# The second tile's instruction order, the place of its output product, and separate buffers for even experts' down weights

## The chip, the cores and the metric

The kernel runs on one core of a Trainium2 chip. The metric is the device time of one execution in microseconds (us), the median of several executions. The engines of the core are TensorE (PE in the rows, PEld for its weight loads), VectorE (DVE), ScalarE (ACT), GpSimd (POOL) and SyncE (SP), which here only issues DMA.

## The reference

One residual stream of 256 tokens with 1024 channels goes through two blocks. The first block ends in a product-key retrieval (128 picked rows per token). The second block is a hybrid layer:

```
def hybrid_layer(x, c, ...):
    mods = jax.nn.silu(c) @ w_ada + b_ada
    h = rms_norm(x, norm1_g) * (1.0 + scale1) + shift1
    proj = h @ w_in                                   # 1824 + 1536 columns
    y_rwkv = rwkv7_time_mix(proj[..., :RWKV_PROJ], ...)  # 8 heads of 64, a scan over tokens
    y_moba = moba_attention(proj[..., RWKV_PROJ:], ...)  # 8 heads of 64, causal softmax
    x = x + gate1 * (jnp.concatenate([y_rwkv, y_moba], axis=-1) @ w_out)
    h = rms_norm(x, norm2_g) * (1.0 + scale2) + shift2
    y = moe_ffn(h, ...)     # 32 experts, top 4 of them per token, each 1024 -> 2048 -> 1024
    return x + gate2 * y
```

Everything is float32. All 32 experts' weights are read once: 8 MB of gate and up weights and 4 MB of down weights for each.

## The kernel before

The 256 tokens are two tiles of 128 rows. Weights stream from HBM in chunks of 1 MB through a ring of 12 slots (`ring`); SP issues every chunk in the order in which TensorE uses it, and waits with each for the chunk that had the slot before (`chunk_done`, counted by TensorE).

The first tile's second block runs between the picks of the second tile's retrieval. When the last pick is done, the second tile's block runs alone: this is the stretch from 912 us to 1104 us, called the bare stretch below. Its work is three programs per engine, written as Python generators that yield the name of their next step: `attention` (steps mb, msum, mscore, mturn, att: the projections for attention, the sums for the norm of q and k, scores, turning of the probabilities, product with v), `mixer` (steps rw, lora, ksum, bonus, gup: its projections and small products; tok, gram, nt: products inside chunks of 32 tokens; pow and inv: powers of a matrix and its inverse; z1, wu, q2, yp, fg, gam: what the scan over chunks needs; st: the scan; ys, ln: output and norm; or: its half of the output product; turn4, route: the router) and `output` (om: the half of the output product that reads attention's result). `to_end` (L205) always takes the program whose next step stands first in the list `ORDER` (L190). So `ORDER` alone sets the order of an engine's instructions in the bare stretch, and since each engine works in order, an instruction that waits holds up all behind it.

In the bare stretch of the kernel before, the rw projections come first, the mb projections stand among the mixer's powers and inverses, the softmax stands beside the scan, and om stands among ln.

After the bare stretch comes the loop over 32 experts (`expert` on TensorE, L2215): 8 gate-up chunks (L2235), gathering the next expert's tokens (L2195), bias rows (L2206), 4 down chunks (L2265), and scattering (L2277). TensorE's first expert waits also for a transfer of bias rows (`loaded_b`, awaited after L2186, issued by ACT at L982 behind its last step of the second tile). SP loads: gate-up of expert 0 into the ring, its four down chunks into `first_dn`, four free pieces of the work buffer `arena`; the down chunks of expert 1 into the ring; then the gate-up of 1, the gate-up and down of 2, of 3, and so on, each chunk into the ring slot that the same chunk of the expert before had.

Of the kernel before, what the change touches and what calls it, by code (L numbers as in the profile page):

```python
# [58 lines left out]


# [24 lines left out]
def stream_order():  # L85
# [103 lines left out]
ORDER = """sum norm gain norm1 xn turn xres rw0.0 rw0.1 rw1.0 rw1.1 mixl rw2.0 rw2.1 loin rw3.0 lora rw3.1 sigw mixk scan rw4.0 rw4.1 ksum kn  # L189
rw5.0 rw5.1 exps mixr kmod rw6.0 rw6.1 rkk rw7.0 bonus rw7.1 mixv gup kk mb0.0 tilde mb0.1 bon mb1.0 mb1.1 tok gram0 gram1  # L190
gram2 gram3 nt mb2.0 pow1 mb2.1 inv1 pow2 mb3.0 inv2 mb3.1 pow3 mb4.0 inv3 mb4.1 pow4 mb5.0 mb5.1 inv4 msq z1 msum wu rms qk
q2 mscore0 yp mscore1 fg0 fg1 fg2 fg3 gam0 gam1 gam2 gam3 soft exp st0 prob st1 mturn0 st2 mturn1 st3 att ys om0 ln1 om1 ln2
om2 ln3 om3 or0 or1 or2 or3 norm2 turn4 route""".split()
# [60 lines left out]
def build(nc, xd, stream, colsd, matsd, rowsd, badad, expert_uv, w_gate_up, w_down, bias_moe, out):  # L254
    with ExitStack() as ctx:
# [149 lines left out]
        first_dn = [area(at, CHUNK) for at in (2048, 4096, 16384, 18432)]  # L405
# [1957 lines left out]
```

## Time and profile before

| | |
|---|---|
| median of 3 executions | 2050.06 us (2047.68 to 2053.04) |
| the profiled execution | 2048.01 us, span 2046.2 us |
| TensorE, VectorE, ScalarE busy | 1767.4, 961.6, 485.8 us |
| HBM read | 770.53 MB, 377 GB/s over the span |
| bare stretch | 912 to 1104 us |
| expert loop | 1104 us to the end |

The span is what the profiler saw of the program; the execution's own time has 1.8 us more around it. The busy shares are means over stages with different limits. In the page's slices the transfers run at 400 to 422 GB/s in most of the program, fall to 42 GB/s in the slices of the bare stretch, and run at 422 GB/s from 1150 us to the end.

### The profile page before, as it was taken

To read this page: it belongs to the slowest core of one execution; us is meant where nothing else is said; L and a number is where in the kernel's file an instruction comes from. 1 tells how busy PE (TensorE), PEld (TensorE's weight loads), DVE (VectorE), ACT (ScalarE), POOL (GpSimd) and SP (SyncE) were. 2 spreads that over 40 slices of the span, in tenths; PEclk is the share of its full clock that TensorE was granted. 3 is DMA by queue.
4 is the path that set the end of the run, shared out by engine and by line. 5 is a ranking of instruction groups with operands and counts; after the bars stand their busy time and mean duration, and the time that the engine had idled before them with its cause. 6 is when DMAs were issued, how large, how long until landed. Compare 5 with 4: busy or idle time off the path is not lost.

```text
span 2046.2 us, 27368 instructions
## 1 busy us (share of the span) xinstructions
PE 1767.4 (86%) x10376; PEld 841.8 (41%) x10376; DVE 961.6 (47%) x2029; ACT 485.8 (24%) x1183; POOL 288.9 (14%) x286
## 2 busy tenths in 40 slices
PE   7999988566688888769967999999999999999997
PEld 6888544111145454318854333333333233333322
DVE  4755877788556776554452223222232232223223
ACT  1111443334345543433221011110111011111101
POOL 1000433334442444320000000000000000000000
PEclk9999998766699998869978999999999999999999
DMA  9982999999999999998217899999999999999997
GB/s 387 388 349 110 387 421 420 421 421 419 420 400 420 413 421 396 367 365 352 91 42 281 347 422 422 422 422 422 422 422 422 422 422 422 422 422 422 422 422 319
DMA packets 107047, 772.69 MB, mean 378 GB/s; under 512 B 12148, under 2 KB 12404, under 8 KB 13272
## 3 DMA queue, kind: packets, MB, share of 16 engines
q1 hardware_dynamic: 69408, 500.51, 59.3%
q0 software_dynamic: 36864, 268.45, 32.0%
q10 hardware_dynamic: 696, 2.66, 0.3%
q8 instruction: 51, 0.84, 0.2%
q14 instruction: 28, 0.23, 0.0%
HBM read 770.53 MB, written 1.05 MB: 377 GB/s over the span
## 4 chain that ended last, share of the span: by engine, by line
PE 50%; DMA 30%; DVE 9%; ACT 4%; SPq 3%; issue 3%; POOL 1%; DVEq 0%; POOLq 0%; ACTq 0%
DMA ring<-in_expert_uv,arena 15%; DMA ring<-in_w_gate_up 14%; PE psum L2235 14%; PE psum L2265 7%; PE psum L1854 6%; PE psum L1706 4%; SPq L605 3%; DVE ring L1275 2%; PE psum L2277 2%; PE psum L1811 2%; PE psum L1956 2%; PE psum L1789 1%; PE psum L1895 1%; PE psum L1774 1%; PE psum L2140 1%
## 5 line engine op out<-in xcount | busy, mean ns | idle before, releaser
L2235 PE MATMUL psum<-ring,arena 128*64 128x512 f32 x2048 | 458.8, 597 | 24.1 <-DMA ring<-in_w_gate_up 22.6
L1854 PE MATMUL psum<-ring,arena 64*64 64x512 f32 x2048 | 348.9, 767 | 145.2 <-ACT arena L837 143.9
L1275 DVE CUSTOM_DVE_ANT_0 ring<-ring,arena 128x1024 f32<-128x1024 f32 x256 | 312.0, 1225 | 164.6 <-DMA ring<-in_expert_uv,arena 162.0
L704 POOL DMA_INDIRECT ring<-in_expert_uv,arena x256 | 278.3, 1087 | 605.5 <-PE psum L1854 399.9
L2235 PEld LDWEIGHTS psum<-ring,arena 128*64 128x64 f32 x2048 | 138.7, 137 | 339.8 <-issue 256.2
L2265 PE MATMUL psum<-ring,arena 128*64 128x512 f32 x992 | 219.7, 595 | 0.6
L1651 DVE TENSOR_SCALAR arena<-psum 128x512 f32<-128x512 f32 x32 | 22.1, 692 | 401.2 <-PE psum L2235 401.2
L1854 PEld LDWEIGHTS psum<-ring,arena 64*64 64x64 f32 x2048 | 64.7, 155 | 349.7 <-ACT arena L837 327.8
L997 ACT ACTIVATE arena<-arena 128x512 f32<-128x512 f32 x32 | 20.2, 630 | 760.2 <-DVE arena L1651 760.2
L828 ACT ACTIVATE arena<-arena 128x1 f32<-128x1 f32 x256 | 51.7, 202 | 328.5 <-DVE arena L1275 328.2
L2265 PEld LDWEIGHTS psum<-ring,arena 128*64 128x64 f32 x992 | 68.5, 137 | 131.9 <-issue 123.9
L1706 PE MATMUL psum<-arena,ring 128*128 128x256 f32 x512 | 111.6, 379 | 0.0
L1660 DVE TENSOR_TENSOR arena<-psum,gates 128x512 f32<-128x512 f32 x32 | 22.1, 691 | 189.4 <-PE psum L2265 189.4
L1706 PEld LDWEIGHTS psum<-arena,ring 128*128 128x128 f32 x512 | 97.0, 190 | 13.2 <-issue 0.4
L1663 DVE TENSOR_TENSOR xres<-xres,psum 128x1024 f32<-128x1024 f32 x64 | 75.3, 1218 | 40.8 <-PE psum L2277 40.8
L837 ACT ACTIVATE arena<-arena 128x64 f32<-128x64 f32 x256 | 89.0, 348 | 8.3
L2277 PE MATMUL psum<-arena 64*128 64x512 f32 x256 | 63.6, 612 | 26.9 <-issue 26.9
L832 ACT ACTIVATE arena<-arena,peer_g 128x1 f32<-128x1 f32 x256 | 75.4, 294 | 8.8
L1811 PEld LDWEIGHTS psum<-arena,ring 128*128 128x128 f32 x512 | 61.2, 197 | 25.3 <-issue 25.3
L1811 PE MATMUL psum<-arena,ring 128*128 128x128 f32 x512 | 66.8, 286 | 0.9 <-ACT arena L737 0.9
L2195 PE MATMUL psum<-arena 128*64 128x512 f32 x264 | 63.8, 605 | 3.3 <-DMA arena<-in_bias_moe 3.3
L1956 PEld LDWEIGHTS psum<-arena,ring 128*128 128x128 f32 x448 | 53.8, 199 | 13.0 <-issue 10.2
(360 smaller groups left out, 1716.7 us busy)
## 6 DMA issues: line engine op xcount, KB each, us to landing
ring<-in_w_gate_up SPq DMA_DIRECT2D x256, 1024.0 KB, 24.8
ring<-in_w_down SPq DMA_DIRECT2D x124, 1024.0 KB, 23.9
ring<-in_stream SPq DMA_DIRECT2D x91, 1024.0 KB, 10.9
ring<-in_expert_uv,arena POOLq DMA_INDIRECT x256, 13.0
arena<-in_w_down SPq DMA_DIRECT2D x4, 1024.0 KB, 6.3
mats<-in_mats ACTq DMA_DIRECT2D x1, 1152.0 KB
xres<-in_x SPq DMA_DIRECT2D x2, 512.0 KB, 4.1
arena<-in_rows ACTq DMA_DIRECT2D x2, 512.0 KB, 7.7
```

What stands on the lines that cost most here:

```text
L704: pool.indirect_dma_start(ring[:, G_SLOTS[b], :], None, expert_uv, bass.IndirectOffsetOnAxis(peer_i[:, tt, k:k + 1], 0)).then_inc(row_in[b ...
L832: act.activation(peer_w[:, 0, c % 4:c % 4 + 1], one, ACT.Copy, scale=peer_g[:, tt, k:k + 1]).then_inc(weight_step, 1)
L837: act.activation(diag[:, c % 4, :], ident2, ACT.Copy, scale=peer_w[:, 0, c % 4:c % 4 + 1]).then_inc(diag_ready, 1)
L1275: dve.tensor_tensor_reduce(u, u, h2[tt], 1.0, 0.0, ALU.mult, ALU.add, peer_h[:, tt, k:k + 1]).then_inc(dot_done, 1)
L1663: dve.tensor_tensor(xres[:, tt, :], xres[:, tt, :], psum[:, (6, 3)[tt]:(8, 5)[tt], :].rearrange("p a c -> p (a c)"), ALU.add).then_inc(acc ...
L1706: last = pe.matmul(psum[:, bank, c * T:(c + 1) * T], wide(n)[:, k, c * P:(c + 1) * P], acts[:, k, :], start=(k == 0), stop=(k == KD - 1))
L1811: last = pe.matmul(psum[:, bank, o:o + P], wide(n)[:, k, cs], h2T[:, k, ts], start=(k == 0), stop=(k == KD - 1), skip_group_check=True)
L1854: last = pe.matmul(psum[o:o + 64, 6 * tt + h, :], diag[rows, c % 4, :], rows_of[b][rows, 1, h * 512:(h + 1) * 512], start=(k == 0), stop=( ...
L1956: last = pe.matmul(half[:, c * P:(c + 1) * P], wide(n)[:, k, c * P:(c + 1) * P], hT3[tt][:, k, :], start=(k == 0), stop=(k == KD - 1), ski ...
L2235: last = pe.matmul(psum[CAP * h:CAP * h + CAP, gu, :], x, w[:, at:at + 512], start=False, stop=(kt == GU_CHUNKS - 1), skip_group_check=True)
L2265: last = pe.matmul(psum[CAP * h:CAP * h + CAP, 5, :], a_in, w[:, i * D + h * 512:i * D + h * 512 + 512], start=False, stop=(kt == KD - 1), ...
L2277: last = pe.matmul(psum[:, (6, 3)[tt] + h, :], sct[rows, tt, :], ye[rows, :], start=True, stop=True)
```

## The change

1. For the second tile the mb projections stream and run before the rw projections, and attention's remaining steps stand between the rw projections.
2. The second tile's om steps stand between the powers and the inverses. Its output product uses PSUM banks 6 and 7 (`OUT_BANK`) where it had 4 and 5, and its wait for `fg_out` goes. Several buffers of the second tile lie elsewhere in `arena` or `mats`.
3. Down chunks of every even expert go to four fixed buffers `more` (the pieces that `first_dn` had), those of odd experts to ring slots. SP issues the chunks in this order: gu0, dn0, dn1, then gu1, dn2, gu2, dn3, gu3, and so on, where gu and dn are the gate-up and the down chunks. TensorE's loop body has two experts.
4. The bias rows' transfer is issued by ACT inside the mixer's step ln2 of the second tile.

```diff
-        seq += rw + mb if tt else mb + rw
-        seq += [("o2", i, tt) for i in range(N_O2)]
+        seq += mb + rw + [("o2", i, tt) for i in range(N_O2)]
...
-ORDER = """sum norm gain norm1 xn turn xres rw0.0 rw0.1 rw1.0 rw1.1 mixl rw2.0 ...
+ORDER = """sum norm gain norm1 xn turn xres mb0.0 mb0.1 mb1.0 mb1.1 mb2.0 ...
...
-            expert(0, 0, range(GU_CHUNKS))
+            gates_ups(0, 0)
             sp.wait_ge(pv_mm, TT)
-            sp.wait_ge(yp_mm, TT)
-            sp.wait_ge(fg_mm, 4 * TT)
             for q in range(DN_CHUNKS):
                 if q == 2:
-                    sp.wait_ge(chunk_done, AT["o2", 0, TT - 1] + 1)
-                down(0, q, first_dn[q]).then_inc(landed_first, 16)
-            expert(1, 0, range(GU_CHUNKS, E_CHUNKS))
-            expert(1, E_CHUNKS, range(GU_CHUNKS))
-            with sp.Fori(2, NE) as e:
-                expert(e, e * E_CHUNKS, range(E_CHUNKS))
+                    sp.wait_ge(fg_mm, 4 * TT)
+                down(0, q, more[q]).then_inc(landed_more[q], 16)
+            for q in range(DN_CHUNKS):
+                n = C_MOE + GU_CHUNKS + q
+                sp.wait_ge(chunk_done, n - SLOTS + 1)
+                down(1, q, slot(n)).then_inc(landed[slot_of(n)], 16)
+            with sp.Fori(0, NE // 2 - 2) as i:
+                for odd in (1, 0):
+                    e = 2 * i + (2 - odd)
+                    gates_ups(e, e)
+                    downs(e + 1, e + 1, 1 - odd)
+            gates_ups(NE - 3, NE - 3)
+            downs(NE - 2, NE - 2, 0)
+            gates_ups(NE - 2, NE - 2)
+            gates_ups(NE - 1, NE - 1)
+            downs(NE - 1, NE - 1, 1)
...
                 yield "ln2"
                 act.wait_ge(ln_mm, 2 * tt + 2)
+                if tt:
+                    act.dma_start(bmoe[0:3 * NE], bias_moe).then_inc(loaded_b, 16)
...
             to_end([started(attention(1)), started(mixer(1))])
-            act.dma_start(bmoe[0:3 * NE], bias_moe).then_inc(loaded_b, 16)
...
                         pe.wait_ge(ym_ready, tt + 1)
-                        pe.wait_ge(fg_out, 4 * (tt + 1))
+                        if tt == 0:
+                            pe.wait_ge(fg_out, 4)
...
-                if isinstance(p, int):
-                    expert(0, 0)
-                with pe.Fori(1 if isinstance(p, int) else 0, NE) as e:
-                    expert(p * NE + e, p * (NE + 1) + e)
+                with pe.Fori(0, NE // 2) as i:
+                    for odd in range(2):
+                        expert(p * (NE // 2) + i, p * (NE + 1) + (2 * i + odd), odd)
```

The line numbers of the changed kernel are up to 22 higher than before for the same code. In TensorE's order of the kernel before, the bare stretch begins with the rw projections (L1956, L1961), with lora (L1969), ksum (L1977) and bonus (L1982) between them:

```order
L1956 MATMUL psum<-arena,ring 128x128 x16
L1961 MATMUL psum<-arena,ring 32x128 x8
L1956 MATMUL psum<-arena,ring 128x128 x32
L1969 MATMUL psum<-arena,mats 128x128 x8
L1956 MATMUL psum<-arena,ring 128x128 x32
L1977 MATMUL psum<-arena,headblk 128x512
L1956 MATMUL psum<-arena,ring 128x128 x32
L1982 MATMUL psum<-arena,headblk 128x512
```

In the changed kernel the mb projections come first (16 and 64 matmuls, not shown), then the same place of TensorE reads as follows; L1977 and L1982 are now rw, L1923 msum, L1935 mscore, L1990 lora, L1946 mturn, L1998 ksum:

```order
L1977 MATMUL psum<-arena,ring 128x128 x16
L1923 MATMUL psum<-arena,headblk 128x512 x2
L1982 MATMUL psum<-arena,ring 32x128 x8
L1935 MATMUL psum<-arena 128x256 x4
L1977 MATMUL psum<-arena,ring 128x128 x8
L1935 MATMUL psum<-arena 128x256 x4
L1977 MATMUL psum<-arena,ring 128x128 x24
L1990 MATMUL psum<-arena,mats 128x128 x8
L1977 MATMUL psum<-arena,ring 128x128 x16
L1946 MATMUL psum<-ident,arena 128x128 x8
L1977 MATMUL psum<-arena,ring 128x128 x8
L1946 MATMUL psum<-ident,arena 128x128 x8
```

The scores and the turning of the probabilities have moved from beside the scan to between the rw projections. TensorE's powers and inverses before, with half mb chunks (L1895) between pow (L2036, L2041) and inv (L2050):

```order
L1895 MATMUL psum<-arena,ring 128x128 x8
L2036 MATMUL psum<-arena 128x128 x4
L2041 MATMUL psum<-arena 128x128 x4
L2036 MATMUL psum<-arena 128x128 x4
L2041 MATMUL psum<-arena 128x128 x4
L1895 MATMUL psum<-arena,ring 128x128 x8
L2050 MATMUL psum<-arena 128x128 x8
```

The same place in the changed kernel, where L2189 is om, L2057 and L2062 pow, L2071 inv:

```order
L2041 MATMUL psum<-arena 128x128 x8
L2057 MATMUL psum<-arena 128x128 x4
L2062 MATMUL psum<-arena 128x128 x4
L2057 MATMUL psum<-arena 128x128 x4
L2062 MATMUL psum<-arena 128x128 x4
L2189 MATMUL psum<-ring,arena 128x256 x4
L2071 MATMUL psum<-arena 128x128 x8
```

One om step now stands between each power and its inverse. On ScalarE, the softmax exponential (L856) before stands directly behind the copy of yp (L939):

```order
L851 ACTIVATE arena<-psum,stat 128x1024
L853 ACT_TABLE_LOAD
L853 ACTIVATE arena<-arena 128x1024
L939 COPY arena<-psum 128x512
L856 ACTIVATE arena<-arena 128x2048
L862 COPY arena<-psum 128x1024 x2
```

In the changed kernel it is L876, and stands behind the copy of an rw chunk pair (L908) and the eight sigmoids of sigw (L926), which read lora's result:

```order
L919 ACTIVATE arena<-arena 32x128
L908 COPY arena<-psum 128x4x128
L926 ACTIVATE arena<-psum,cols 128x128 x8
L876 ACT_TABLE_LOAD
L876 ACTIVATE arena<-arena 128x2048
L882 COPY arena<-psum 128x1024 x2
```

A load of the activation table now stands between the sigmoids and the exponential.

## Rows read from the trace of the kernel before

**Rows 1.** Windows: microseconds, then busy time (instructions) by engine, clock, DMA share, GB/s.
```profile
1025.00:1050.00 25.00, 10.54 (x246) 9.19 (x242) 17.62 (x27) 2.50 (x2) 0.00 (x0) 0.64 0.01 1
...
1500.00:2000.00 500.00, 464.46 (x2250) 154.24 (x2252) 136.43 (x237) 57.76 (x85) 0.00 (x0) 1.00 1.01 422
```

**Rows 2.** Chain of waits, expert loop: start, duration, what.
```profile
1103.82 13.98 PE psum L2235 x64
...
1122.04 7.09 PE psum L2265 x32
...
1131.96 13.91 PE psum L2235 x64
```

**Rows 3.** Windows around the first expert.
```profile
1125.00:1130.00 5.00, 4.16 (x22) 1.21 (x18) 0.69 (x1) 0.00 (x0) 0.00 (x0) 1.00 0.46 192
1130.00:1135.00 5.00, 5.00 (x24) 1.83 (x26) 3.35 (x7) 0.00 (x0) 0.00 (x0) 1.00 0.00 0
1135.00:1140.00 5.00, 5.00 (x26) 1.67 (x24) 0.00 (x0) 0.00 (x0) 0.00 (x0) 1.00 0.89 310
```

**Rows 4.** Timeline, TensorE: start, duration, line, shapes, records; in brackets idle before and releaser.
```profile
926.56 5.25 PE L1956 MATMUL psum<-arena,ring 128*128 128x128 f32 x32 [2.20 <-ACT arena L880]
...
942.03 7.41 PE L1956 MATMUL psum<-arena,ring 128*128 128x128 f32 x64
...
961.51 7.17 PE L1891 MATMUL psum<-ring,arena 128*128 128x256 f32 x32
968.52 1.91 PE L1999 MATMUL psum<-ident,arena 128*128 128x128 f32 x16
...
979.30 1.16 PE L2036 MATMUL psum<-arena 128*128 128x128 f32 x8 [0.97 <-DVE arena L1476]
...
1013.71 1.99 PE L1902 MATMUL psum<-arena,headblk 128*128 128x512 f32 x4 [0.25 <-DVE arena L1288]
...
1023.59 1.14 PE L1914 MATMUL psum<-arena 64*128 64x256 f32 x8 [2.50 <-DVE arena L1293]
...
1038.80 1.94 PE L2113 MATMUL psum<-mats,arena 128*128 128x64 f32 x8 [5.69 <-issue]
...
1056.60 3.24 PE L1934 MATMUL psum<-arena 128*64 128x128 f32 x32 [1.10 <-ACT arena L862]
1059.77 0.42 PE L2124 MATMUL psum<-arena,mats 64*64 64x32 f32 x8
...
1061.75 2.00 PE L2167 MATMUL psum<-ring,arena 128*128 128x256 f32 x8
...
1073.36 8.61 PE L2140 MATMUL psum<-ring,arena 128*128 128x256 f32 x32 [2.60 <-DVE arena L1551]
...
1097.23 3.39 PE L2195 MATMUL psum<-arena 128*64 128x512 f32 x8 [3.33 <-DMA arena<-in_bias_moe]
```

**Rows 5.** Timeline, ScalarE.
```profile
942.13 2.17 ACT L906 ACTIVATE arena<-psum,cols 128x128 f32<-128x128 f32 x8 [0.50 <-PE psum L1969]
...
1016.86 1.28 ACT L853 ACT_TABLE_LOAD   x1
1018.16 1.06 ACT L853 ACTIVATE arena<-arena 128x1024 f32<-128x1024 f32 x1
...
1043.38 1.91 ACT L856 ACTIVATE arena<-arena 128x2048 f32<-128x2048 f32 x1 [14.81 <-DVE arena L1310]
```

**Rows 6.** Timeline, VectorE.
```profile
1045.32 2.29 DVE L1314 TENSOR_REDUCE gsm<-arena 128x8 f32<-128x2048 f32 x1 [1.19 <-ACT arena L856]
...
1053.83 0.42 DVE L1527 TENSOR_TENSOR arena<-psum,arena 128x256 f32<-128x256 f32 x1 [2.87 <-PE psum L2113]
...
1094.53 0.42 DVE L1612 TENSOR_SCALAR arena<-iota_slot,arena 128x64 f32<-128x64 f32 x2
```

**Rows 7.** Windows of 5 us: the clock where TensorE resumes.
```profile
1025.00:1030.00 5.00, 5.00 (x110) 4.23 (x107) 1.83 (x6) 0.58 (x1) 0.00 (x0) 0.66 0.00 0
...
1050.00:1055.00 5.00, 4.78 (x23) 4.78 (x24) 1.78 (x5) 1.01 (x1) 0.00 (x0) 0.50 0.00 0
```

More of the change, by code:

```diff
@@ L58 @@
 FG_BANK = (4, 5, 1, 2)
+OUT_BANK = (4, 6)
 N_Z = D_IN // CW
@@ L186 @@
 assert max(SLOT.values()) < PICKS
[L189 to L193, printed above, removed]
+ORDER = """sum norm gain norm1 xn turn xres mb0.0 mb0.1 mb1.0 mb1.1 mb2.0 mb2.1 mb3.0 mb3.1 mb4.0 mb4.1 mb5.0 mb5.1 msq
+rw0.0 rw0.1 msum rms rw1.0 qk rw1.1 mixl mscore0 rw2.0 loin mscore1 rw2.1 lora sigw soft rw3.0 rw3.1 exp mixk rw4.0 prob rw4.1
+scan ksum kn mturn0 rw5.0 mturn1 rw5.1 exps mixr kmod att rw6.0 rw6.1 rkk rw7.0 bonus rw7.1 kk tilde mixv gup bon tok gram0
+gram1 gram2 gram3 nt pow1 om0 inv1 pow2 om1 inv2 pow3 om2 inv3 pow4 om3 inv4 z1 wu q2 yp fg0 fg1 fg2 fg3 gam0 gam1 gam2 gam3
+st0 st1 st2 st3 ys ln1 ln2 ln3 or0 or1 or2 or3 norm2 turn4 route""".split()
 RANK = {s: i for i, s in enumerate(ORDER)}
@@ L403, in build @@
         gmoe = gates[:, 1, 0:512]
-        first_dn = [area(at, CHUNK) for at in (2048, 4096, 16384, 18432)]
+        more = [area(at, CHUNK) for at in (16384, 18432, 2048, 4096)]
         xs = area(6144, W2)
@@ L608, in down, with gates_ups @@
                 return sp.dma_start(dst, w_down[e, q * 2 * P:(q + 1) * 2 * P, :].rearrange("(p k) c -> p (k c)", k=2))
-            def expert(e, before_it, js):
-                for j in js:
+            def gates_ups(it, e):
+                for j in range(GU_CHUNKS):
                     n = C_MOE + j
-                    sp.wait_ge(chunk_done, before_it + (n - SLOTS + 1))
-                    if j < GU_CHUNKS:
-                        ins = gate_up(e, j, slot(n))
-                    else:
-                        ins = down(e, j - GU_CHUNKS, slot(n))
-                    ins.then_inc(landed[slot_of(n)], 16)
@@ L623, in _, with downs @@
-            expert(0, 0, range(GU_CHUNKS))
+                    sp.wait_ge(chunk_done, it * E_CHUNKS + (n - SLOTS + 1))
+                    gate_up(e, j, slot(n)).then_inc(landed[slot_of(n)], 16)
+            def downs(it, e, odd):
+                for q in range(DN_CHUNKS):
+                    n = C_MOE + GU_CHUNKS + q
+                    sp.wait_ge(chunk_done, it * E_CHUNKS + (n - 2 * E_CHUNKS + 1))
+                    if odd:
+                        down(e, q, slot(n)).then_inc(landed[slot_of(n)], 16)
+                    else:
+                        down(e, q, more[q]).then_inc(landed_more[q], 16)
@@ new lines, in _ @@
+            for q in range(DN_CHUNKS):
+                n = C_MOE + GU_CHUNKS + q
+                sp.wait_ge(chunk_done, n - SLOTS + 1)
[8 more added lines that the diff above has]
+            gates_ups(NE - 2, NE - 2)
@@ L636, in experts @@
+            gates_ups(NE - 1, NE - 1)
+            downs(NE - 1, NE - 1, 1)
             def experts(p):
-                with sp.Fori(0, NE) as e:
-                    expert(e, e * E_CHUNKS + p * (NE * E_CHUNKS), range(E_CHUNKS))
+                with sp.Fori(0, NE // 2) as i:
+                    for odd in range(2):
+                        gates_ups(p * NE + (2 * i + odd), 2 * i + odd)
+                        downs(p * NE + (2 * i + odd), 2 * i + odd, odd)
             further_passes(sp, experts)
@@ L2139, in mixer @@
                     for k in range(4):
-                        last = pe.matmul(psum[:, 4 + n // 2, (n % 2) * CW:(n % 2 + 1) * CW], yT[tt][:, k, :],
+                        last = pe.matmul(psum[:, OUT_BANK[tt] + n // 2, (n % 2) * CW:(n % 2 + 1) * CW], yT[tt][:, k, :],
                                          wide(AT["o2", n, tt])[:, k, :], start=False, stop=(k == 3), skip_group_check=True)
```

33 lines of the change are left out of this document (17 added, 16 removed).

## The prediction

> **What bounds the kernel now.** I read the windows first. In the expert loop the transfers run at 422 GB/s without a hole [rows 1], so from there on HBM sets the pace. A 1 MB chunk then takes 1.0486 MB / 422 GB/s = 2.485 us, an expert's twelve 29.8 us. The chain of waits shows TensorE's own pace, which is faster: first gate-up matmul of expert 0 at 1103.82, of expert 1 at 1131.96, so 28.14 us each [rows 2]. In the bare stretch the transfers nearly stop (0.01 of the engines' time between 1025 and 1050 [rows 1]): the buffers for weights are full and free up only when TensorE reaches expert 0. So the end is the moment T0 of expert 0's first matmul (1103.8 before), plus the holes in the transfers after T0, plus a fixed number of chunks, plus a tail (last down chunk, scatter, store) that the change leaves as it is. Everything before 923 us is also left as it is. Two questions remain: what happens to T0, and to the holes.
>
> **The hole behind T0.** Before T0, 16 chunks are loaded (gu0, dn0, dn1) in both kernels. From T0 on gu1 follows as gu0 is consumed. Before, gu2 stood next, and had to wait for gu1's slots, thus until T0 + 28.1 + 1.75: the windows show the transfers ending near 1127.3 (0.46 of 1125 to 1130), none from 1130 to 1135, and a start near 1135.55 (0.89 of the next) [rows 3]. The hole is 8.25 us. In the changed kernel dn2 stands behind gu1 and goes where dn0 was, which TensorE consumes from 1122.04, that is T0 + 18.2 [rows 2]: its first chunk is free at T0 + 20, before gu1 is in at T0 + 23.5. Its four chunks take 9.9 us, until T0 + 33.4, and by T0 + 29.9 gu2 may start. The hole closes: -8.25 us. After that TensorE's slack only grows (1.7 us per expert), so the 16 buffers bring nothing more. The loop body of two experts costs or saves nothing while HBM sets the pace.
>
> **T0: the bare stretch, leg by leg.** TensorE is the engine to follow; the section on the change has its order. Times are on the clock of the trace before; both kernels start at 926.56.
>
> Leg 1, to tok. Before, tok starts at 968.52 [rows 4]. Now:
> - mb: two chunks of v 7.1 (their row), plus 1.6 which the first 32 records lost at the low clock (5.25 where 3.65 is normal); four of k and q at 3.65, less overlap 14.3; rw0 3.7: 953.3 [rows 4].
> - msum to mscore. Before, msum started at 1013.71 and mscore at 1023.59, but VectorE was held there by other work. Without that: Ln ready 2.0 + 1.1, table load and Exp 2.4, VectorE 1.5: 7.05 [rows 4, 5]. So mscore0 starts at 960.35; only 1.9 us of rw1 lie in it, TensorE idles 3.4.
> - mscore0, rw2.0, a wait of 0.7 for VectorE's reading of the scores, mscore1: 965.0. rw2.1 to rw3.1 5.4, lora 1.1, rw4 3.6: 975.1.
> - mturn0 needs the probabilities. The scores are reduced and ready for the exponential at 971.2, but on ScalarE it stands behind sigw: lora starts at 970.4, its first result allows sigw at 971.6, sigw takes 2.2, the table load 1.3, Exp 1.9: 977.0 [rows 5]. VectorE's reduce, reciprocal, multiply: 4.9 (from 1045.32 to TensorE's next at 1050.2) [rows 6]. So mturn0 starts at 982.0, and behind it all of TensorE's queue (rw5 to gup) has waited 6.9 us.
> - mturn, rw5, ksum, att 3.2 (L1934), rw6, rw7, bonus, gup: 22.7. After such an idle stretch the granted clock was 0.50 to 0.66 of full speed for the next 5 us or more [rows 7], and full again before 10 us of work; I take 2.5 us for it (bounds 0 and 4.4). ScalarE's copy of gup's result 0.7: tok at 1007.9. That is +39.4.
>
> Leg 2, tok to the first scan step. Before 968.52 to 1038.80, 70.3 us [rows 4]. Now tok to pow1 10.8 as before (968.52 to 979.30, VectorE's masks set it). A level of powers is 3.6 of pow and 1.8 of inv, and om's 1.75 stands between them. I looked for slack there and found none: pow's copies are ready when inv wants them, so om's four steps cost their full 7 us, where before, between ln steps (1061.75 on), they lay in waits and cost about 0.3. Three levels of 7.2 and one of 5.4: 27.0. z1 and its copy 2.7, wu 4.5, q2 1.0, yp 3.2, fg 4.1, gam 5.5. From z1 on these are the distances in TensorE's timeline before, without mscore's share. Sum 58.8: the scan starts at 1066.7. That om no longer waits for `fg_out` and has banks of its own is what lets it stand here, and is worth nothing by itself.
>
> Leg 3, the scan to ys (L2124). Before 1038.80 to 1059.77, 21.0 us, because softmax, turning and att stood in it. Now three steps of 1.85 + 0.87 + 0.1 (1051.98 to the next VectorE row at 1053.83, and its two operations) [rows 6]: 8.5. ys at 1075.2.
>
> Leg 4, ys to or. Before 1059.77 to 1073.36, 13.6 us [rows 4]. TensorE now comes to it from 15 us of little work, without om between, and so at the low clock: ys, two sums for the norm and the first of or lengthen. 13.6 - 0.3 + 2.5 = 15.8 (bounds 13.3 and 17): or at 1091.0.
>
> Leg 5, or to T0. Before 30.5 us. The bias rows landed at 1097.23, while the one-hot rows that L2195 also needs were written by 1094.95 [rows 4, 6]: moving the transfer up is worth 2.3 us and no more; its issue (0.1 to 0.3) now stands ahead of ln2's Ln. The low clock adds 0.8 to or. 29.2: T0 at 1120.2, so +16.4.
>
> In short, and roughly: stalls removed beside the scan and softmax are worth 12.5 in leg 3, and are paid for by attention's 6.8 us of products moved ahead, om's 7, two new stalls of 3.4 and 6.9, 1.8 of filler gone from gram, and clock. The bounds on T0 are +10.5 (no clock cost at all: 2.5, 2.5 and 0.8 less) and +20 (both clock terms at their upper ends).
>
> **The sum.** 2048.0 (the profiled execution) + 16.4 - 8.25 = 2056.2. The median of the runs shown is 2.0 above that execution: 2058. Transfers do not spoil it: the second tile's output chunks are in by 970, long before om, and dn1 is in 12 us after or starts, with 29 us until T0.
>
> At the table load the trace shows the next activation 0.02 us behind the load's 1.28 [rows 5], and I used that. The Trainium skill (ScalarE: Activation LUTs, What ACT_TABLE_LOAD costs) adds a drain of about 1.38 us to each switch. By that rule the load that now stands before the softmax exponential, on the path, would cost 1.4 us more, an estimate of 2059.6; the trace disagrees with it here.
>
> **Rivals.**
> - No measurable change. The clock does not matter: the windows mix idle time and low clock, and the small products of leg 4 may be bound by their fixed cost. Then T0 is +10 to +12, the sum 2050 + 2 to +4: 2053. For it: the products of leg 4 are few and stand between VectorE's steps. Against: 0.50 in every row where TensorE resumed late [rows 7]. Chance 0.27.
> - Faster. What is bought: TensorE's waits of 5.69 before the scan, 2.50 and others beside softmax (about 21 us between 1013 and 1062) go, and the new ones do not appear: if probabilities are ready before rw4 ends, 10.3 of stalls and 2.5 of clock go from my sum, and if om finds 7 us of slack in the powers, that too. T0 is -3, and with the hole 2058 - 20 = 2038. It decides at mturn0: the exponential would have to end by 970. Against: ScalarE's order puts sigw first, and no duration in the chain is uncertain by more than tenths. Chance 0.09.
> - Much slower. TensorE's clock stays low through rw5 to gup and from the scan until T0: another 5 to 10 us, 2066. Chance 0.05.
>
> **How the numbers follow.** My case 0.59, at 2058, its own range 2054 to 2062. Range 2049 to 2064. About 0.3% (6 us) can be told from no change: slower means above 2056.2. Of my case 0.57 lies above it and 0.02 below; with the last rival slower is 0.62. Same is 0.27 + 0.02 = 0.29, faster 0.09.
>
> **What the changed profile would show.** TensorE: a wait of about 7 us before the first mturn (L1946), one of 3.4 before the first mscore (L1935); no idle time around om (L2189) among the powers, and pow1 to z1 27 us; the scan's three steps in 8.5 us; expert 0's first matmul near 1120, 16 later. Transfers: no window without traffic between T0 + 5 and T0 + 40. No wait for the bias rows. I am wrong in the mechanism if the exponential starts before lora's sigmoids or T0 is earlier than 1112; wrong in the loop if a hole remains, or if the end does not follow T0.

## The result: slower by 1.3%, outside the range

| | before | after |
|---|---|---|
| median | 2048.87 us (4 executions, 2047.01 to 2053.04) | 2074.94 us (4 executions, 2073.31 to 2078.73) |
| the profiled execution | 2048.01 | 2078.73 |
| bare stretch, first projection to T0 | 926.56 to 1103.82 = 177.3 | 927.87 to 1132.67 = 204.8 |
| T0 to TensorE's last group (scatter of expert 31) | 933.2 | 933.4 |
| T0 to the end of the span | 942.4 | 944.2 |
| mean clock in the bare stretch | 0.87 | 0.78 |

The ratio is 1.0127 (95% interval 1.0105 to 1.0149). The forecast was 2058 with a range up to 2064. The profiled execution is the slowest of its four, 3.8 us above their median, so sizes read from it are a little large.

The profile has two places to read. The first is the bare stretch: TensorE's timeline after, with start, duration, line, shapes and records, and in brackets the idle time before and its releaser. These rows answer to [rows 4].

```profile
927.87 9.42 PE L1912 MATMUL psum<-ring,arena 128*128 128x256 f32 x32 [2.20 <-ACT arena L900]
...
961.89 1.14 PE L1935 MATMUL psum<-arena 64*128 64x256 f32 x8 [3.16 <-DVE arena L1314]
...
984.67 1.97 PE L1946 MATMUL psum<-ident,arena 128*128 128x128 f32 x8 [6.60 <-DVE arena L1337]
...
1010.58 3.68 PE L2020 MATMUL psum<-ident,arena 128*128 128x128 f32 x16 [3.36 <-DVE arena L1471]
...
1023.20 1.16 PE L2057 MATMUL psum<-arena 128*128 128x128 f32 x8 [2.95 <-DVE arena L1497]
...
1042.67 1.89 PE L2189 MATMUL psum<-ring,arena 128*128 128x256 f32 x8
1044.40 1.95 PE L2071 MATMUL psum<-arena 128*128 128x128 f32 x16
...
1055.44 0.64 PE L2088 MATMUL psum<-arena 128*128 128x64 f32 x2
...
1073.95 1.94 PE L2134 MATMUL psum<-mats,arena 128*128 128x64 f32 x8 [5.64 <-issue]
...
1083.09 3.62 PE L2145 MATMUL psum<-arena,mats 64*64 64x32 f32 x64 [1.07 <-DVE mats L1550]
...
1091.90 2.07 PE L2155 MATMUL psum<-arena,headblk 128*128 128x512 f32 x2 [1.59 <-DVE arena L1562]
1101.69 9.54 PE L2161 MATMUL psum<-ring,arena 128*128 128x256 f32 x32 [7.72 <-DVE arena L1572]
...
1124.79 3.68 PE L2217 MATMUL psum<-arena 128*64 128x512 f32 x8 [1.19 <-DVE arena L1633]
1128.40 2.00 PE L2228 MATMUL psum<-arena 32*64 32x512 f32 x12
...
1132.67 3.65 PE L2257 MATMUL psum<-ring,arena 128*64 128x512 f32 x16 [1.67 <-DVE arena L1650]
```

The two stalls that the prediction named are there, before mscore (L1935, 3.16) and before mturn (L1946, 6.60). So is om (L2189) among the powers with no wait beside it. Nobody waits for the bias rows: L2217 waits 1.19 for VectorE. New are the 3.36 before tok (L2020), and the length of everything at the end: TensorE waits 7.72 before or (L2161) where it waited 2.60, or took 9.54 where it took 8.61, L2217 3.68 for 3.39 and L2228 2.00 for 1.10.

The windows after (microseconds, busy time by engine, clock, DMA share, GB/s) show the clock that goes with it; compare the clock of [rows 7].

```profile
1050.00:1055.00 5.00, 4.12 (x38) 4.02 (x37) 2.07 (x3) 0.00 (x0) 0.00 (x0) 1.00 0.00 0
1055.00:1060.00 5.00, 5.00 (x27) 5.00 (x26) 0.69 (x1) 0.00 (x0) 0.00 (x0) 0.53 0.02 3
...
1095.00:1100.00 5.00, 0.00 (x0) 0.00 (x0) 1.62 (x5) 4.55 (x5) 0.00 (x0) 0.50 0.27 78
1100.00:1105.00 5.00, 3.31 (x8) 2.68 (x9) 1.57 (x3) 0.00 (x0) 0.00 (x0) 0.50 0.00 0
...
1125.00:1130.00 5.00, 5.00 (x20) 0.93 (x18) 1.06 (x6) 1.73 (x3) 0.00 (x0) 0.50 0.00 0
...
1155.00:1160.00 5.00, 4.16 (x22) 1.50 (x20) 0.69 (x1) 0.00 (x0) 0.00 (x0) 1.00 1.00 415
1160.00:1165.00 5.00, 5.00 (x26) 1.62 (x24) 3.35 (x7) 0.00 (x0) 0.00 (x0) 1.00 1.01 421
```

The granted clock is at its lower level (0.50, which is 1.2 of 2.4 GHz) in most windows from 1055 to 1130. The last two rows are the place that answers to [rows 3], 22 to 32 us behind T0: the transfers run at 415 and 421 GB/s there. The hole of 8.25 us is gone. Yet from T0 on nothing was gained: the end is 1.8 us later. For that, the second place: TensorE at the loop's end, after.

```profile
2023.53 1.94 PE L2257 MATMUL psum<-ring,arena 128*64 128x512 f32 x8 [0.54 <-DMA ring<-in_w_gate_up]
...
2039.73 13.95 PE L2257 MATMUL psum<-ring,arena 128*64 128x512 f32 x64
...
2066.02 1.99 PE L2299 MATMUL psum<-arena 64*128 64x512 f32 x8 [0.84 <-issue]
```

And the same place before:

```profile
1993.03 1.94 PE L2235 MATMUL psum<-ring,arena 128*64 128x512 f32 x8 [0.54 <-DMA ring<-in_w_gate_up]
...
2009.15 10.69 PE L2235 MATMUL psum<-ring,arena 128*64 128x512 f32 x48
2020.38 1.94 PE L2235 MATMUL psum<-ring,arena 128*64 128x512 f32 x8 [0.54 <-DMA ring<-in_w_gate_up]
2022.86 1.94 PE L2235 MATMUL psum<-ring,arena 128*64 128x512 f32 x8 [0.55 <-DMA ring<-in_w_gate_up]
...
2037.06 1.99 PE L2277 MATMUL psum<-arena 64*128 64x512 f32 x8 [0.84 <-issue]
```

Before, TensorE waits for the last gate-up chunk of expert 31 (2022.86), 14.2 us ahead of its last group, the scatter. After, its last wait is for the last gate-up chunk of expert 30 (2023.53), and from there TensorE's own pace sets the 42.5 us to the scatter: expert 31's 64 matmuls run without a wait. Before, the same way took 44.0, so TensorE had 1.5 us of slack there. In the new order dn30 stands ahead of gu30, and every gate-up from expert 2 on is four chunks (9.9 us) later in the queue. Measured from T0, the last chunk of gu30 came at 1993.03 - 1103.82 = 889.2 before and at 2023.53 - 1132.67 = 890.9 after: -8.25 for the hole, +9.94 for the four chunks, +1.69 in all. The slack takes 1.5 of it, and the scatter starts 0.1 later, at T0 + 933.4 for 933.2.

The rest of the 1.8 is the store of the output, which SP issues in

```profile
2070.77 0.83 SPq L663 DMA_DIRECT2D out<-xres  x2
```

after, 6.1 us ahead of the span's end, and before in

```profile
2041.81 0.83 SPq L643 DMA_DIRECT2D out<-xres  x2
```

4.4 us ahead of it. From the scatter to the end of the span it is 9.1 to 10.5 us in the five kernels of this document with the old loads, and 9.9 to 11.1 in the eight with new ones. Whether the loads or chance make this difference is not settled.

### The profile page after: what moved, and what is told of

Its sections match the earlier page's. It is cut to its first block, busy times and chain, and to the rows that moved or that the text cites. A ratio compares the mean times of both kernels' runs of the same rounds, so it can differ in the third digit from the quotient of the medians.

```text
span 2076.9 us, 27251 instructions
## 1 busy us (share of the span) xinstructions
PE 1779.7 (86%) x10376; PEld 854.7 (41%) x10376; DVE 962.2 (46%) x2029; ACT 485.4 (23%) x1183; POOL 286.9 (14%) x286
## 4 chain that ended last, share of the span: by engine, by line
PE 51%; DMA 28%; DVE 9%; ACT 5%; issue 3%; SPq 3%; POOL 0%; ACTq 0%; DVEq 0%; POOLq 0%
DMA ring<-in_expert_uv,arena 15%; DMA ring<-in_w_gate_up 14%; PE psum L2257 14%; PE psum L2287 7%; PE psum L1727 5%; PE psum L1875 5%; SPq L609 3%; DVE ring L1296 2%; PE psum L2299 2%; PE psum L1832 2%; PE psum L1977 2%; PE psum L1810 1%; PE psum L1916 1%; PE psum L1795 1%; PE psum L2161 1%
## 5 line engine op out<-in xcount | busy, mean ns | idle before, releaser
L2257 PE MATMUL psum<-ring,arena 128*64 128x512 f32 x2048 | 457.1, 597 | 23.6 <-DMA ring<-in_w_gate_up 21.9
L2257 PEld LDWEIGHTS psum<-ring,arena 128*64 128x64 f32 x2048 | 138.9, 137 | 337.3 <-issue 263.6
L2287 PE MATMUL psum<-arena 128*64 128x512 f32 x512 | 113.4, 595 | 1.6
L2287 PE MATMUL psum<-ring,arena 128*64 128x512 f32 x512 | 113.4, 595 | 1.5
L1727 PEld LDWEIGHTS psum<-arena,ring 128*128 128x128 f32 x512 | 96.8, 190 | 13.3 <-issue 0.4
L1832 PEld LDWEIGHTS psum<-arena,ring 128*128 128x128 f32 x512 | 61.0, 196 | 24.8 <-issue 24.8
L2217 PE MATMUL psum<-arena 128*64 128x512 f32 x264 | 64.0, 607 | 1.2 <-DVE arena L1633 1.2
L2287 PEld LDWEIGHTS psum<-arena 128*64 128x64 f32 x512 | 36.5, 137 | 68.1 <-issue 68.1
## 6 DMA issues: line engine op xcount, KB each, us to landing
ring<-in_stream SPq DMA_DIRECT2D x91, 1024.0 KB, 10.5
```

The costliest lines, as they stand in the source:

```text
L1727: last = pe.matmul(psum[:, bank, c * T:(c + 1) * T], wide(n)[:, k, c * P:(c + 1) * P], acts[:, k, :], start=(k == 0), stop=(k == KD - 1))
L1832: last = pe.matmul(psum[:, bank, o:o + P], wide(n)[:, k, cs], h2T[:, k, ts], start=(k == 0), stop=(k == KD - 1), skip_group_check=True)
L2217: last = pe.matmul(psum[CAP * h:CAP * h + CAP, 2, :], oh[:, tt, :], xn4[:, tt, h * 512:(h + 1) * 512], start=(tt == 0), stop=(tt == TT - 1))
L2257: last = pe.matmul(psum[CAP * h:CAP * h + CAP, gu, :], x, w[:, at:at + 512], start=False, stop=(kt == GU_CHUNKS - 1), skip_group_check=True)
L2287: last = pe.matmul(psum[CAP * h:CAP * h + CAP, 5, :], a_in, w[:, i * D + h * 512:i * D + h * 512 + 512], start=False, stop=(kt == KD - 1), ...
```

## Experiments

Times are medians; ratios are to the kernel before in the same batch, with 95% intervals. 1 us is 0.0005. The changed kernel ran in the batch of the result alone, so differences to it compare medians across batches; the kernel before had 2048.87 there, 2049.01 with e1 to e4, 2048.73 with e5 to e9 and 2047.81 with e10 to e12. Stretch means first projection to T0 in the profiled execution, "to the end" T0 to the end of the span, "to the scatter" T0 to TensorE's last group.

**e1_loop_only and e2_loop_switch: does the loop's change lose its gain to the place of the down chunks?** e1 is the kernel before with part 3 of the change alone. e2 closes the hole in the same way, but SP goes back to gate-up first in the middle of the loop:

```
-            with sp.Fori(0, NE // 2 - 2) as i:      # e1, as in the change
+            with sp.Fori(0, 7) as i:                # e2
                 for odd in (1, 0):
                     e = 2 * i + (2 - odd)
                     gates_ups(e, e)
                     downs(e + 1, e + 1, 1 - odd)
...
+            gates_ups(15, 15)
+            with sp.Fori(8, NE // 2) as i:
+                for odd in range(2):
+                    gates_ups(2 * i + odd, 2 * i + odd)
+                    downs(2 * i + odd, 2 * i + odd, odd)
```

> The kernel before with part 3 of the change alone (down chunks of even experts in their own buffers, SP's new order, loop body of two experts). Both theories leave the bare stretch and the first expert's start as they are. Recorded theory (only the hole counts): the hole of 8.25 us behind the first expert closes and the rest is fixed, so 8 us faster, 2041. New theory (end of the loop): the hole closes, but every gate-up from expert 2 on now stands behind the four down chunks of its own expert, 4 x 2.49 = 10.0 us of transfer that was behind it before. From the arrival of expert 30's last gate-up chunk TensorE alone needs 53 us to the end, so the end moves by 10.0 - 8.25 = +1.7: 2050.6, from 0 to 3 us slower.

> As the kernel with part 3 alone, but SP returns at expert 16 to the order gate-up of an expert, then its down chunks (gate-up of 15, gate-up of 16, down of 16, gate-up of 17, down of 17, ...). New theory: the hole stays closed, and at the end a gate-up has no down chunk of its own ahead of it; the limit is again expert 31's last gate-up chunk, 23.3 us before the end: 7 to 8 us faster than the kernel before, 2041. Recorded theory: 2041 too, and the same as part 3 alone. A third possibility, that the closed hole is lost elsewhere (TensorE's loop, contention): the same as part 3 alone, at 2049 or later.

Measured: e1 2051.35, ratio 1.0015 [1.0001, 1.0029], 945.2 to the end, 934.9 to the scatter. e2 2043.01, ratio 0.9972 [0.9959, 0.9985], 936.2 to the end, 926.4 to the scatter. The recorded theory that the closed hole gives 8 us fell with e1; the new theory's times held for e1 and nearly for e2 (6 us gained, 7 to 8 expected). Its 53 us from gu30's last chunk to the end are TensorE's 42.5 and the way from the scatter to the end; it left out the 1.5 of slack. At the end of the loop of e2, the last gate-up chunk of expert 31 is again the last wait:

```profile
2018.54 1.94 PE L2254 MATMUL psum<-ring,arena 128*64 128x512 f32 x8 [0.57 <-DMA ring<-in_w_gate_up]
```

It is at T0 + 912.1, where before it was at 2022.86 - 1103.82 = 919.0: 6.9 earlier, not 8.25. In both profiled executions the granted clock was low in the first microseconds behind T0 (0.50 from 1107.5 to 1110 in e2), and expert 0's 64 gate-up matmuls took 15.65 us instead of 13.95; SP's first chunk behind T0 was issued at T0 + 3.4 in e2 and T0 + 3.3 in e1, where before it was T0 + 2.0. That accounts for the missing 1.4. The same delay is in e1's 934.9, where the changed kernel has 933.4. In e10 below, which has e2's loads and took 13.95 for these matmuls, the scatter is at T0 + 924.8, 8.5 earlier than before: the whole hole. So the early down chunks are worth 6 us by medians if the order goes back once the hole is behind, and nothing if it stays.

**e3_bias_only: part 4 alone.**

```
                 yield "ln2"
...
+                if tt:
+                    act.dma_start(bmoe[0:3 * NE], bias_moe).then_inc(loaded_b, 16)
...
-            act.dma_start(bmoe[0:3 * NE], bias_moe).then_inc(loaded_b, 16)
```

> The kernel before with part 4 alone (the bias rows' transfer issued inside ln2). Recorded theory: 2.3 us of waiting gone less 0.1 to 0.3 for the issue: 2 us faster, 2047. New theory: ScalarE's table load for Ln, which before was done while it waited for ln2's sum, now stands behind the issue of the transfer, on the path: 0.34 + 1.28 later there, so only 0.7 us faster, 2048, and a trace in which the load of L942's table starts after the transfer's issue. The hole in the transfers stays 8.25 us.

Measured: 2050.45, ratio 1.0010 [0.9997, 1.0022]. Stretch 179.7, which is 2.4 longer than before. ScalarE in e3:

```profile
1067.97 0.34 ACTq L943 DMA_DIRECT2D arena<-in_bias_moe  x1
1068.34 1.28 ACT L944 ACT_TABLE_LOAD   x1 [7.25 <-PE psum L2135]
1069.64 0.69 ACT L944 ACTIVATE arena<-psum,stat 128x512 f32<-128x512 f32 x1
```

and before, where the load of Ln's table is over before its data is there:

```profile
1060.49 1.28 ACT L942 ACT_TABLE_LOAD   x1
...
1067.35 0.69 ACT L942 ACTIVATE arena<-psum,stat 128x512 f32<-128x512 f32 x1 [5.58 <-PE psum L2134]
```

The issue stands behind the wait for the sum of the norm, and the table load behind the issue. Both are now on the path: or in e3 is

```profile
1075.64 9.75 PE L2141 MATMUL psum<-ring,arena 128*128 128x256 f32 x32 [4.26 <-DVE arena L1552]
```

It waits 4.26 for VectorE where it waited 2.60 [rows 4], 1.66 more, and then runs 9.75 long at the low clock where it ran 8.61. These two are 2.8 us. The gather behind then waits 1.19 for VectorE instead of 3.33 for the bias rows, 2.1 less, but it and the bias rows' products take 3.68 and 2.00 instead of 3.39 and 1.10, 1.2 more. So nothing is gained. Both expectations, 2 and 0.7 us faster, missed, the second narrowly: the interval reaches from 0.6 us faster to 4.5 slower. By the Trainium skill (ScalarE: Activation LUTs, What ACT_TABLE_LOAD costs) a drain of about 1.38 us would follow the load; here the activation starts 0.02 us behind it.

**e4_order_only: parts 1 and 2 alone.** The changed kernel's `ORDER`, stream order, banks and buffers, with the loads, the loop and the bias rows of before:

```
+OUT_BANK = (4, 6)
...
-        seq += rw + mb if tt else mb + rw
-        seq += [("o2", i, tt) for i in range(N_O2)]
+        seq += mb + rw + [("o2", i, tt) for i in range(N_O2)]
```

> The changed kernel with the loads and the loop of the kernel before (its experts' order, first_dn) and the bias rows issued where they were: parts 1 and 2 alone. Recorded theory: the bare stretch is 18.5 us longer (16.4 + 2.3 - 0.2), 2067. New theory from the trace of the changed kernel: the order costs all that was measured, +26 less what parts 3 and 4 do (+1.7 and -0.7), so +25: 2074. Both expect the loop behind the first expert as before.

Measured: 2068.58, ratio 1.0095 [1.0077, 1.0112], stretch 200.2, 943.2 to the end. The order costs 19.5 us (15.8 to 22.9). That is the recorded theory's 18.5; the new theory's 25 fell. In the profiled execution the stretch is 22.9 longer than before, but it began 3.5 earlier; its start lies anywhere from 921.7 (e1) to 928.5 (e11) in the profiled executions, which the medians carry too. With e1's 3 and e3's 2 the parts sum to about 25 of the 26 measured.

e4 also shows what part 4 does once the order has changed. Its bias rows are issued where they were before, behind or, and still nobody waits for them:

```profile
1094.00 8.60 PE L2141 MATMUL psum<-ring,arena 128*128 128x256 f32 x32 [6.05 <-DVE arena L1552]
...
1115.71 3.68 PE L2197 MATMUL psum<-arena 128*64 128x512 f32 x8 [1.19 <-DVE arena L1613]
```

Their transfer landed 4.4 us after its issue, against 9.6 in the kernel before. So the wait of 3.33 that part 4 was to remove was gone by the order alone. What was left of part 4 is its price: in the changed kernel TensorE waits 7.72 before or for 6.05 here, and or takes 9.54 for 8.60.

**e5_om_back: does om cost its full 7 us among the powers?** The changed kernel, om back at ys and ln:

```
- gram1 gram2 gram3 nt pow1 om0 inv1 pow2 om1 inv2 pow3 om2 inv3 pow4 om3 inv4 z1 wu ...
+ gram1 gram2 gram3 nt pow1 inv1 pow2 inv2 pow3 inv3 pow4 inv4 z1 wu ...
- st0 st1 st2 st3 ys ln1 ln2 ln3 or0 ...
+ st0 st1 st2 st3 ys om0 ln1 om1 ln2 om2 ln3 om3 or0 ...
```

> The changed kernel with the second tile's four om steps back at their old place, behind ys, ln1, ln2 and ln3, and nothing else moved. Theory (as recorded: among the powers they fill no waits and cost their full 1.75 us each): pow1 to z1 7 us shorter, and between ln steps they lie in TensorE's waits of 1.5, 1.6 and 7.7 us and keep its clock up there, worth 1 to 3 us more: 8 to 10 us faster than the changed kernel, 2066. Rival (the powers wait for their copies anyway, om fills that): no change, 2075.

Measured: 2069.64, ratio 1.0102 [1.0088, 1.0117], so 5.3 us less than the changed kernel. Stretch 197.6, 7.2 less. Its pow1 and z1 start at 1020.02 and 1041.45, 21.4 apart; in the changed kernel 1023.20 and 1051.49, 28.3. The step of the prediction is shown right: om costs its full length there. The 1 to 3 us more that the expectation gave to the clock did not come.

**e7_no_turn_stall: the stall before the turning.** The changed kernel; on ScalarE the exponential comes before the sigmoids, and the two mturn and att stand one projection later:

```
- ... lora sigw soft rw3.0 rw3.1 exp mixk rw4.0 prob rw4.1
- scan ksum kn mturn0 rw5.0 mturn1 rw5.1 exps mixr kmod att rw6.0 rw6.1 rkk rw7.0 bonus ...
+ ... lora soft rw3.0 rw3.1 exp sigw mixk rw4.0 prob rw4.1
+ scan ksum kn rw5.0 rw5.1 mturn0 exps mixr kmod rw6.0 mturn1 rw6.1 rkk rw7.0 att bonus ...
```

> The changed kernel with an order of the second tile in which ScalarE does the softmax exponential ahead of sigw, and TensorE the turning of the probabilities behind rw5 and rw6 and att behind rw7.0. Theory: TensorE's wait of 6.6 us in front of the first turning goes, and with it the half clock behind it (1.6 us): 7 to 8 us faster than the changed kernel, 2067. Rival: VectorE and ScalarE, not TensorE, set the end of this leg (the products before tok wait for VectorE's mixv, kk and tilde): the wait only moves to tok, under 3 us faster.

Measured: 2063.72, ratio 1.0072 [1.0056, 1.0089], 11.2 us less than the changed kernel. Stretch 190.4. The 6.60 is gone, and 1.35 before att is all that came in its place; tok starts 8.6 us earlier, counted from the first projection (74.1 for 82.7):

```profile
989.27 1.97 PE L1955 MATMUL psum<-arena 128*64 128x128 f32 x32 [1.35 <-ACT arena L882]
1000.71 3.67 PE L2020 MATMUL psum<-ident,arena 128*128 128x128 f32 x16 [3.36 <-DVE arena L1471]
```

The forecast was 7 to 8 us, the gain 11.2 (14.4 in the profiled stretches). Up to tok it is 8.6, for the stall and the low clock behind it. The other 5.7 of the stretch lie between tok and the scan (57.7 for 63.4), where nothing was moved: in e7 the first powers and the products of wu and q2 ran at the higher level, in the changed kernel for the most part at the lower one. That the stall is the cause of this part too is not shown.

**e8_warm: what the low clock costs.** The changed kernel with extra 128x128 products of constants, whose result nobody reads, in TensorE's waits: 18 before the first mturn, 8 before tok and before pow1, 2 before wu, 12 before the scan, 2 to 3 between its steps and in ys and ln, 18 before or, 14 and twice 4 about the router. Each is sized to the wait that it fills.

```
+            def warm(n, bank):
+                for _ in range(n):
+                    pe.matmul(psum[:, bank, 0:P], headblk[:], ident[:], start=True, stop=True)
```

> The changed kernel with extra TensorE products (128x128x128, results unused) inside TensorE's waits of the second tile: 18 before the first turning, 8 before tok, 8 before pow1, 2 before wu, 12 before the first scan step, 2 before each next one and ys, 3 before each of the ln sums, 18 before or, 14 before turn4, 4 and 4 before the last two waits. Clock theory: what T0 was later than recorded is for the most part TensorE's low clock behind its waits (turning and rw5, wu, scan, ys, ln sums, or, gathering); kept busy, it stays at full clock there: 6 to 9 us faster than the changed kernel, 2067, with the mean granted clock of the bare stretch up from 0.78 to over 0.9. Rival (work, not the clock): the extra products help nothing and where they overrun a wait cost up to 5 us: 2075 to 2080.

Measured: 2062.81, ratio 1.0070 [1.0055, 1.0085], 12.1 us less (6 to 9 were expected), with 100 products added and none of the work changed. Stretch 186.6 for 204.8; this profiled execution is 4.0 below its median and that of the changed kernel 3.8 above, so the difference of 18.2 is too large. The windows of the two bare stretches (the changed kernel, then e8):

```profile
927.00:1133.00 206.00, 158.76 (x1246) 138.06 (x1248) 80.52 (x170) 43.66 (x69) 0.00 (x0) 0.78 0.37 142
```

```profile
926.00:1112.00 186.00, 165.93 (x1444) 148.48 (x1444) 79.35 (x165) 43.06 (x67) 0.00 (x0) 0.93 0.40 156
```

The clock rises from 0.78 to 0.93, and TensorE's rows shorten; or and the gather in e8:

```profile
1088.47 7.17 PE L2188 MATMUL psum<-ring,arena 128*128 128x256 f32 x32 [3.70 <-DVE arena L1572]
...
1107.64 1.94 PE L2248 MATMUL psum<-arena 128*64 128x512 f32 x8
1109.50 1.10 PE L2259 MATMUL psum<-arena 32*64 32x512 f32 x12
```

against 9.54, 3.68 and 2.00 above. The rival, that the extra products help nothing, fell: the low clock's cost is measured here, not argued.

**e12_bias_late, e11_bias_late_warm, e9_before_best: the kernel before, with what was learned.** e12 issues the bias rows inside ln2, but behind its Exp. e11 adds extra products ahead of or and about the router. e9 has both and the loads of e2.

```
                 # e12, e11, e9: ScalarE, ln2: Ln, Exp, and then
+                if tt:
+                    act.dma_start(bmoe[0:3 * NE], bias_moe).then_inc(loaded_b, 16)
...
                 # e11, e9: TensorE, ahead of or
+                    if tt and n == 0:
+                        warm(8, bank_late)
                 # ahead of turn4, and 4 each ahead of L2185 and L2195
+                if tt:
+                    warm(14, bank_late)
```

> The kernel before with one thing changed: the rows of the gate's bias are issued behind the Exp of ln2 and not at their place before. If the bias rows' place alone gave e9 its shorter end of stretch, 2046 to 2047 (the gather then waits for no DMA: 2.3 us less). If the clock gave it, no change, 2048 to 2049.

> The kernel before with its bias rows issued behind the Exp of ln2, and unused TensorE products ahead of or and in the waits behind turn4; the loop is untouched. Of the 10.5 us that e9_before_best gained, the loop's part was 6 (e2). Theory (the rest is clock and table load at the stretch's end): stretch 172 as in e9, about 2044. Rival (e9 gained by its loop, and by more than e2): stretch 177, 2049.

> The kernel before with three things: the loads of the loop that switch at expert 16, the bias rows' transfer issued by ScalarE behind the exponential of ln2 (no table load behind it), and extra TensorE products with unused results in its late waits (8 before or, 14 before turn4, 4 and 4 before the last two waits). Theory: -6 as measured for the loads, -2.3 for the bias rows, -2 to -3 for the clock from or to the first expert: 2038. Rival: the extra products delay what stands behind them and the bias rows' wait was covered: -5 to -6, 2043.

Measured (e11 and e9 as expected, their rivals fell): e12 2045.87, ratio 0.9991 [0.9981, 1.0001], stretch 176.5. e11 2044.34, ratio 0.9977 [0.9968, 0.9986], stretch 172.2. e9 2038.25, ratio 0.9949 [0.9936, 0.9962], stretch 172.0, 936.8 to the end. In e12 the gather starts with no wait for a DMA, as hoped, but it and the bias rows' products run at the low clock, where before they caught the higher one (3.39 [rows 4] and 1.10):

```profile
1095.77 3.68 PE L2196 MATMUL psum<-arena 128*64 128x512 f32 x8 [1.19 <-DVE arena L1613]
1099.38 2.00 PE L2207 MATMUL psum<-arena 32*64 32x512 f32 x12
```

So only 0.8 of 2.3 us is left in the stretch, and the time can't be told from no change. With the extra products of e11 the same rows take:

```profile
1095.32 2.11 PE L2208 MATMUL psum<-arena 128*64 128x512 f32 x8
1097.36 1.10 PE L2219 MATMUL psum<-arena 32*64 32x512 f32 x12
```

**e10_changed_best: the changed kernel with every repair.** The orders of e5 and e7 in one, the loads of e2, the bias rows as in e12, extra products as in e8 but none before the first mturn and in ln, and with 10 ahead of or (68 in all):

```
+ ... lora soft rw3.0 rw3.1 exp sigw mixk ... rw5.0 rw5.1 mturn0 exps mixr kmod rw6.0 mturn1 rw6.1 rkk rw7.0 att ...
+ ... pow1 inv1 pow2 inv2 pow3 inv3 pow4 inv4 z1 wu ... ys om0 ln1 om1 ln2 om2 ln3 om3 or0 ...
...
-            with sp.Fori(0, NE // 2 - 2) as i:
+            with sp.Fori(0, 7) as i:
```

> The changed order with every repair together: second tile's sigmoid behind ScalarE's exp and the turn of the hidden rows one projection later (worth 10 us and more in e7), om back at ys and ln1 to ln3 (5 to 7 us, e5), SyncE back to gate-up first from expert 16 (8 us, e2), the bias rows issued behind ln2's Exp, and unused TensorE products in the waits of the stretch (12 us and more, e8). Theory (the loss is the sum of these separate costs, and the order itself is then worth something): stretch 172 to 176 us, T0 to the end 937, so about 2038 to 2041, level with e9_before_best (2038). Rival (the costs overlap, the same clock loss counted in e7 and e8 alike): stretch 180 or more, about 2046.

Measured: 2037.40, ratio 0.9944 [0.9932, 0.9957], stretch 175.2, 934.9 to the end. The theory (2038 to 2041) held, the rival of 2046 fell: the repairs of e5, e7, e8 and e2, measured alone as 5.3, 11.2, 12.1 and about 8.3 (e1 to e2), sum to 37; e10 is 37.5 below the changed kernel. The sum leaves out the bias rows, which e10 also repairs (e3 to e12: 3.9 us by ratios), and e8's products before mturn, which e10 lacks, so a small overlap of the costs is not excluded. e10 and e9 are level in time. That the two orders themselves are worth the same is not shown by this: e9 has 30 extra products, all from or on, and its waits beside the scan are not filled; its stretch is 3.2 shorter than that of e10, and it is 1.0 longer from T0 to the scatter and 0.9 from there to the end. What is shown is that the changed kernel with these repairs comes level with e9.

## Why the prediction was wrong

It missed by 16.9 us. The direction was right. The parts of the change, measured alone, show where the miss lies (us, by ratios, with 95% intervals; the forecasts are those of the prediction's sum):

| part | forecast | measured |
|---|---|---|
| 1 and 2, the order (e4) | +18.5 | +19.5 (15.8 to 22.9) |
| 3, the loads (e1) | -8.25 | +3.1 (0.2 to 5.9) |
| 4, the bias rows (e3) | -2.1 | +2.0 (-0.6 to +4.5) |

So the step that failed is the loop's, with 11 us, and then the bias rows, with 4. The order's total was near by medians. In the profiled stretches it is 4.4 off (22.9 for 18.5), and the changed kernel takes another 4.6 over e4, 3.4 of it from ys on, where part 4 stands and 2.1 were to be gained.

- **"A tail ... that the change leaves as it is": wrong, worth 8.4 us to the scatter, 11 by e1's ratio.** The step took the end as T0 plus holes plus a fixed number of chunks. The hole did close. But the end hangs on the last gate-up chunk that TensorE waits for, plus what it must still do behind it, and the change moved every gate-up from expert 2 on behind its own expert's down chunks. The clue was in the trace before, not looked up: TensorE needs 28.1 us per expert where the chunks come every 29.8, so only 1.7 us of slack lie between gu30 and the end. gu30 can't be 9.9 us later in the queue unseen. The line "the 16 buffers bring nothing more" asked what more buffers give and not what their order takes.
- **The clock: mis-sized, 5.8 us taken.** e8 shows 12 us by medians. The kernel before also loses some, at its end alone 1.5 by medians and 4.3 in the profiled stretches (e11 against e12; its other waits were not filled), so the change adds at most some 8 to 11. The two places that the prediction named were right, but it let the clock recover in time for all of leg 2 and for leg 5. Instead it was low at tok, at the first powers and at wu, ran at half level through the scan and norm, and again from 1115 to 1130. The rival "much slower" described part of this and got 0.05. The prediction also says 0.50 "in every row"; [rows 7] has 0.66 and 0.50.
- **Bias rows: 2.3 gain forecast, none came** (e3). The price of the issue was set at 0.1 to 0.3 us; it was 0.34. What was missed is the hidden table load behind it, the low clock of the gather, and that in the new order nobody waits for these rows anyway (e4).
- **tok: 3.36 not foreseen.** On VectorE mixv, which needs the last rw chunk, stands ahead of kk and tilde inside the program of the mixer, and tok needs those. Before, four half mb chunks of products lay over it. Leg 1 was still only 1.4 off (82.7 from the start for 81.3), and that is luck: the first mturn to the end of gup took 22.5 where 25.2 was forecast, among it 3.2 for att, a row read at the low clock, which took 1.97.
- **Right:** the stalls of 3.4 and 6.9 (3.16 and 6.60), om's full 7 (e5), no wait for om, the scan in 8.5 (9.1), the closed hole.

By legs, measured less forecast: tok +1.4, scan start +4.6, ys +0.6, or +2.8, T0 +1.8: 11.2 in the profiled execution. Of the 4.6, 1.8 lie between tok and pow1, 1.3 among the powers and 1.5 behind z1; of the 2.8 before or, 1.7 are the bias rows' issue and table load, by the distance from ys to or in e4 (16.9 for 18.6). The stretch also began 1.3 later (927.87 for 926.56), from T0 to the scatter it is 8.4 off, and from there to the end, with the store, 1.7: 22.5 in all for the profiled execution. The forecast stood 2.0 above its own, and the one after lies 3.8 above its median, which leaves the 16.9.

The Trainium skill (TensorE: Matmul & The Clock Gate, Part 1) puts the penalty of the clock's ramp under 1% of a typical kernel's span. Here the extra products of e8 won back 12.1 of 2075 us, 0.6%: inside that bound, and yet twice what this measurement can tell from no change.

## What to carry to other kernels

When a fetch order changes in a loop that the transfers bound, find the last wait for a transfer, and add up the compute behind it: closing a hole early is worth nothing if the chunk that this wait needs moves back in the queue. Price a new stall on TensorE at more than its length, and try extra products in its waits. A wait that an experiment removes in the kernel before may be gone in the changed one; look there too. Before something is put in front of an instruction that waits, look for what is being hidden in that wait, a table load above all.

## What the runs showed of the hardware

The clock fell without a long wait. In the changed kernel it was at 1.00 in the windows from 1045 to 1055, with TensorE busy 4.12 to 5.00 of each 5 us, and at 0.53 in the next; what stood there were z1's 64-column products (1051.49), a wait of 0.88 us, and the first products of wu. It isn't settled what decides this: in e8 wu ran at the higher level with two extra products ahead of it and others further up, and in e7 it did with none at all, the mixer's rows from z1 on and the wait being the same. The first two products of wu take the same in both kernels, the fifth pair shows the fall. The changed kernel:

```profile
1054.26 0.41 PE L2086 MATMUL psum<-arena 128*128 128x64 f32 x2 [0.88 <-DVE arena L1517]
...
1055.17 0.48 PE L2086 MATMUL psum<-arena 128*128 128x64 f32 x2
1055.44 0.64 PE L2088 MATMUL psum<-arena 128*128 128x64 f32 x2
```

and e7, where all of wu stays at 0.39:

```profile
1043.21 0.41 PE L2086 MATMUL psum<-arena 128*128 128x64 f32 x2 [0.88 <-DVE arena L1517]
...
1044.12 0.39 PE L2086 MATMUL psum<-arena 128*128 128x64 f32 x2
```

At the end of the stretch 0.50 stayed through a 5 us window in which TensorE was busy 5.00 (1125 to 1130). A load of the activation table took 1.28 us, and in e3 the next activation started 0.02 us behind it. The bias rows' transfer (384 KB) landed 9.6 us after its issue in the kernel before, where the windows from 1085 to 1095 show 426 and 343 GB/s of traffic, 4.4 in e4, and 3.3 in the changed kernel, where it was issued at 1094.02 with next to no other traffic (1 GB/s from 1090 to 1095).
